# The output projection of three pooling groups: seven block products in the place of eight

## The chip, the cores and the metric

The kernel runs on one core of a Trainium2 chip. The metric is the device time of one execution in microseconds (us); the number that counts is the median of several runs.

## The reference

The reference is a two-part network in float32 on 1024 tokens of width 1024. The part that matters here is the pooling mixer of the second block, which has four groups of 512 channels:

```python
def pool_mixer(h, w_in, w_group, scale, w_out):
    u, z = jnp.split(h @ w_in, 2, axis=-1)
    p = causal_multiscale_pool(u).reshape(B, S, N_POOL_GROUPS, GROUP_WIDTH)
    y = jnp.einsum('bsgc,gcd->bsgd', p, w_group).reshape(B, S, A_WIDTH_2) * scale
    return (y * jax.nn.silu(z)) @ w_out
...
    x = x + gate[:, None, :] * y
```

After the mixer, the keys and values of an attention layer are made from the new x: an RMS norm over x, a modulation, and a product with w_kv. That stage is called the key stage here.

## The kernel before

Activations lie transposed: 128 channels on the partitions, 1024 tokens along the free dimension, so x is 8 tiles (xT, tile o). TensorE multiplies in a 32-bit format that rounds its inputs, so each float32 operand is split in a high part (a rounded copy) and a low part (the rest), and each product of a 128x128 weight block with 512 tokens is three matmuls: high by high, high by low, low by high (`product`, L705, L706, L708). The high part of a weight block is a cast on ScalarE (`group_high`, L2884), the low part a subtraction on GpSimd (`group_low`, L1658). Weights come in strips by SyncE's DMA queue (`load_group_half`, L1434) into `raw`, two slots of two halves, and each half is loaded again once the low part made from it is there.

The pooling groups g = 1, 2, 3 run one after the other. In each, work goes by forms: a form is four 128x128 weight blocks, split into one of four places of split_hi and split_lo (form p uses place p % 4, so the split of form p waits until TensorE has done form p - 4). A group has 40 forms:

- Forms 0 to 27, the input projection, in four quads of seven (`pool_quad`). Each quad does a 2x2 block product with seven products in the place of eight (the Strassen-Winograd scheme): sums of weight blocks are made on GpSimd (L1672, L1674, L1677, L1679), sums of the token blocks were made once, and VectorE adds the seven results up (L3655 to L3675). A form is 12 matmuls of 512 tokens. The low part of the seventh form of each quad is made by VectorE (`plain_low`, L3684); the last half strip of the quad's weights can be overwritten only after it.
- Forms 28 to 31, the group's own square matrix, one tile of 1024 tokens each, 24 matmuls. VectorE multiplies the result with the gate (`gate_product`, L3589), ScalarE casts the high part (L2834), VectorE makes the low part (`gate_low`, L3594).
- Forms 32 to 39, the output projection, one tile of x each: 4 blocks of channels by 1024 tokens, 24 matmuls. VectorE adds each to x (`residual`, L3607). In the last group ScalarE squares and splits each finished tile of x for the key stage (L481, L564), and VectorE adds the squares and makes the low parts between the residuals (L488, L581).

The order on every engine is the order in the program. ScalarE waits in `group_high` for the place to come free, GpSimd waits for ScalarE's cast, SyncE waits for the low part. Tiles 6 and 7 of x lie in DRAM while a group runs, and ScalarE's queue brings them back (`x_pair_d`).

## Time and profile before

| | us |
|---|---|
| median of 3 runs (2353.84 to 2354.54) | 2354.03 |
| the profiled execution | 2353.32 |
| its span in the profile | 2351.4 |
| TensorE busy in the span | 2324.9 |
| VectorE busy | 1537.1 |
| ScalarE busy | 859.8 |
| GpSimd busy | 1255.9 |

Around the span lie 1.9 us. TensorE's granted clock is at full speed throughout (0.999). A matmul's entry is 0.39 us long, but matmuls overlap: what one costs in a stream is the distance from its start to the next one's. Groups 1 to 3 run from 1513 to 1946 us.

### The profile page before, as it was taken

How to read it: one execution, taken by the hardware profiler on the slowest of the kernel's cores; microseconds unless marked ns; L12 is line 12 of the kernel's file. 1: busy time of each engine (PE TensorE's matmuls, PEld its weight loads, DVE VectorE, ACT ScalarE, POOL GpSimd, SP SyncE). 2: the span in 40 equal slices, each digit the busy share in tenths (PEclk: the TensorE clock that was granted, in tenths of full speed). 3: DMA queues.
4: the chain of work that ended last, by engine and by line, in shares of the span. 5: the costliest groups of instructions: out<-in, count | busy, mean ns of one | idle time of the engine just before them, and what ended most of it. 6: DMA issues, size and time to landing. Idle time of an engine off the chain costs nothing.

```text
span 2351.4 us, 32286 instructions
## 1 busy us (share of the span) xinstructions
PE 2324.9 (99%) x11585; PEld 1943.6 (83%) x11585; DVE 1537.1 (65%) x1839; ACT 859.8 (37%) x1596; POOL 1255.9 (53%) x724
## 2 busy tenths in 40 slices
PE   9999999999999999999999999999999999999998
PEld 7888789888888888888888888788878788889887
DVE  7825555524578777877877777774672967147885
ACT  5212555512543222222222443122231244157773
POOL 4533954143135666676777424573754733467743
PEclk9999999999999999999999999999999999999999
DMA  6511001031011333333332211112121123210034
GB/s 220 157 45 50 19 19 37 1 117 54 10 42 50 117 125 125 117 124 125 117 123 63 63 45 45 59 57 73 54 81 62 58 67 110 79 37 25 22 112 139
DMA packets 67420, 179.08 MB, mean 76 GB/s; under 512 B 7010, under 2 KB 13924, under 8 KB 65200
## 3 DMA queue, kind: packets, MB, share of 16 engines
q1 hardware_dynamic: 57840, 148.03, 19.3%
q10 hardware_dynamic: 9104, 27.51, 3.5%
q0 software_dynamic: 368, 2.10, 0.5%
q8 instruction: 68, 1.11, 0.2%
q14 instruction: 40, 0.33, 0.0%
HBM read 161.84 MB, written 15.77 MB: 76 GB/s over the span
## 4 chain that ended last, share of the span: by engine, by line
PE 76%; DVE 6%; issue 4%; POOL 2%; ACT 1%; DMA 0%; POOLq 0%; DVEq 0%; ACTq 0%; SPq 0%
PE ps L705 21%; PE ps L706 21%; PE ps L708 21%; PE ps L855 4%; PE ps L833 3%; PE ps L843 2%; DVE trail L3538 1%; PE ps L2410 1%; POOL split_lo L1658 1%; PE ps L2426 1%; ACT p L956 1%; PE ps L2395 1%; PE ps L2396 1%; PE ps L2425 1%; PE ps L509 0%
## 5 line engine op out<-in xcount | busy, mean ns | idle before, releaser
L705 PE MATMUL ps<-h_hi,split_hi 128*128 128x512 f32 x1546 | 607.2, 393 | 3.4 <-DVE h_lo L3220 1.3
L706 PE MATMUL ps<-h_lo,split_hi 128*128 128x512 f32 x1546 | 601.9, 389 | 0.0
L708 PE MATMUL ps<-h_hi,split_lo 128*128 128x512 f32 x1546 | 536.5, 389 | 0.0
L1516 POOL TENSOR_TENSOR split_hi<-raw,cf 128x1024 fp32r<-128x1024 f32 x64 | 125.2, 1956 | 427.8 <-PE ps L708 373.2
L705 PEld LDWEIGHTS ps<-h_hi,split_hi 128*128 128x128 f32 x1546 | 290.9, 188 | 63.9 <-issue 2.2
L708 PEld LDWEIGHTS ps<-h_hi,split_lo 128*128 128x128 f32 x1546 | 290.9, 188 | 61.0
L706 PEld LDWEIGHTS ps<-h_lo,split_hi 128*128 128x128 f32 x1546 | 291.2, 188 | 56.3 <-issue 0.2
L1605 POOL TENSOR_TENSOR split_lo<-raw,split_hi 128x512 fp32r<-128x512 f32 x144 | 232.9, 1635 | 193.9 <-ACT split_hi L2723 193.4
L1658 POOL TENSOR_TENSOR split_lo<-raw,split_hi 128x512 fp32r<-128x512 f32 x84 | 128.1, 1534 | 179.2 <-ACT split_hi L2884 179.2
L2723 ACT CAST split_hi<-raw 128x512 fp32r<-128x512 f32 x144 | 86.7, 622 | 283.9 <-PE ps L708 204.0
L1518 POOL TENSOR_TENSOR split_lo<-raw,split_hi 128x1024 fp32r<-128x1024 f32 x64 | 178.4, 2787 | 5.0
L705 PE MATMUL ps<-act_hi,split_hi 128*128 128x512 f32 x320 | 125.5, 392 | 1.5 <-DVE xT L3443 1.4
L706 PE MATMUL ps<-act_lo,split_hi 128*128 128x512 f32 x320 | 124.8, 390 | 0.0
L3760 DVE CUSTOM_DVE_ANT_0 p<-ps,swa_bias,sink_row 128x256 f32<-128x256 f32 (+1 forms) x128 | 54.6, 464 | 102.8 <-PE ps L2396 102.3
L2884 ACT CAST split_hi<-raw 128x512 fp32r<-128x512 f32 x96 | 58.2, 620 | 138.8 <-PE ps L708 128.4
L3443 DVE TENSOR_TENSOR xT<-xT,ps 128x1024 f32<-128x1024 f32 x72 | 87.4, 1214 | 30.6 <-PE ps L708 30.5
L3313 DVE SCALAR_TENSOR_TENSOR ada_acc<-ada_raw,cact,ada_acc 128x1024 f32<-128x1024 f32 x56 | 102.6, 1832 | 0.8
L705 PE MATMUL ps<-p_hi,split_hi 128*128 128x512 f32 x256 | 99.9, 390 | 0.5 <-DVE pool_tmp L3665 0.5
L706 PE MATMUL ps<-y_lo,split_hi 128*128 128x512 f32 x256 | 99.8, 390 | 0.0
L708 PE MATMUL ps<-act_hi,split_lo 128*128 128x512 f32 x320 | 98.7, 390 | 0.0
L705 PE MATMUL ps<-sum_hi,split_hi 128*128 128x512 f32 x240 | 93.7, 390 | 0.3 <-ACT quad_tmp L2748 0.3
L706 PE MATMUL ps<-sum_lo,split_hi 128*128 128x512 f32 x240 | 93.6, 390 | 0.0
(508 smaller groups left out, 5213.2 us busy)
## 6 DMA issues: line engine op xcount, KB each, us to landing
raw<-in_strips SPq DMA_DIRECT2D x208, 256.0 KB, 2.8
raw<-in_strips SPq DMA_DIRECT2D x86, 512.0 KB, 3.4
ada_raw<-in_ada SPq DMA_DIRECT2D x64, 512.0 KB, 3.7
memw_raw<-in_mem_strips SPq DMA_DIRECT2D x8, 512.0 KB, 6.1
xT<-in_xT ACTq DMA_DIRECT2D x4, 1024.0 KB, 8.1
x_spill_d<-xT ACTq DMA_DIRECT2D x1, 3584.0 KB, 10.1
xT<-x_spill_d ACTq DMA_DIRECT2D x2, 1792.0 KB, 9.9
out_T<-out_sb SPq DMA_DIRECT2D x13, 256.0 KB, 2.2
```

The lines of the kernel that those rows point to most:

```text
L705: pe.matmul(acc[:, a:b], w_hi, hi[:, a:b], start=first, stop=False)
L706: pe.matmul(acc[:, a:b], w_hi, lo[:, a:b], start=False, stop=False)
L708: mm = pe.matmul(acc[:, a:b], w_lo, hi[:, a:b], start=False, stop=last)
L833: mm = pe.matmul(at[:, lo:hi], q, k, start=j == 0, stop=j == len(group) - 1)
L855: mm = pe.matmul(o, a["pt"][:, w % 4, j * P:(j + 1) * P], unit["values"][b0 + j], start=b0 + j == 0, stop=b0 + j == nblk - 1)
L1516: pool.tensor_tensor(hi, raw[:, r, :], ones[:, 0:1].to_broadcast([P, D]), ALU.mult).then_inc(hi_split, 1)
L1518: pool.tensor_tensor(lo, raw[:, r, :], rows(hi), ALU.subtract).then_inc(split_ready[r], 1)
L1605: pool.tensor_tensor(form_tiles(split_lo, p), src, rows(form_tiles(split_hi, p)), ALU.subtract).then_inc(form_ready, 1)
L1658: pool.tensor_tensor(group_tiles(split_lo, p), src, rows(group_tiles(split_hi, p)), ALU.subtract).then_inc(form_ready, 1)
L2723: act.copy(form_tiles(split_hi, p), src).then_inc(form_hi, 1)
L3313: dve.scalar_tensor_tensor(out=ada_acc[:, :], in0=ada_raw[:, r, :], scalar=cact[:, k:k + 1], in1=ada_acc[:, :], op0=ALU.mult, op1=ALU.add) ...
L3443: dve.tensor_tensor(xT[:, o, :], xT[:, o, :], pair(2 + o % 2), ALU.add).then_inc(ffn_res, 1)
```

## The change

In groups 1 to 3 the output projection is done in two quads of seven forms (`out_form`), each for four tiles of x, in the place of eight forms. The 4 channel tiles of the group are two pairs, the tokens two halves, and a quad's four tiles of x two pairs; a form is two parts (one for each tile of a pair), each of 2 blocks by 512 tokens, 12 matmuls in all. A group has 46 forms. Some forms add onto a PSUM bank that was read before (`start=i in (0, 1, 3)`).

New on each engine, per group:

- GpSimd: the low parts of 12 forms and four sums in each quad (`out_forms`), where there were 8 low parts. The second form of a quad is the low part of a sum of both halves of the second strip.
- ScalarE: 14 weight casts in the place of 8, the casts of the token sums in halves (`out_high`, `neg_high_tile`), in group 3 the key stage's squares and splits at other places (`key_square`).
- VectorE: the token differences (`first_difference`, `neg_two`, `neg_three`, `neg_four`), their low parts, 28 additions of 512 tokens to x (`out_sum`) in the place of 8 of 1024, and the low part of each quad's seventh form (`plain_low`). In group 3, the squares' additions and the low parts of the key stage.
- In groups 1 and 2 the token sums lie where half of the tiles 0 to 5 of h was. Those halves are saved to DRAM in group 1 (`h_keep_d`), and in the next group they come back on ScalarE's DMA queue (`h_fetch`) and ScalarE rounds them again (`h_round`, six casts), for which the sixth and seventh form wait.
- SyncE loads the last half strip of a quad after its sixth and seventh form are split (`load_out`). The strips of the output weights are packed in another order.
- The loops over groups on TensorE, GpSimd and SyncE are written out.

```diff
+            def load_out(g, quad):
+                for i, d in ((2, 0), (3, 1), (4, 2), (6, 3)):
+                    if d == 3:
+                        group_split(sp, g, out_form(quad, 5))
+                    group_split(sp, g, out_form(quad, i))
+                    load_group_half(g, 12 + 2 * quad + d // 2, d % 2)
...
+            def out_forms(g, quad):
+                j, at = 10 + 2 * quad, out_form(quad, 0)
+                group_half(pool, g, j, 0)
+                group_low(g, at, OUT_SOURCE[0])
+                group_half(pool, g, j + 1, 0)
+                group_half(pool, g, j + 1, 1)
+                pool.tensor_tensor(pool_form, a21, a22, ALU.add).then_inc(form_sum, 1)
+                group_low(g, at + 1, OUT_SOURCE[1])
+                summed(g, 4 + quad, 1)
+                pool.tensor_tensor(a21, a21, a11, ALU.subtract).then_inc(form_sum, 1)
+                group_split(pool, g, at + 1)
+                pool.tensor_tensor(pool_form, a11, pool_form, ALU.subtract).then_inc(form_sum, 1)
+                group_low(g, at + 2, OUT_SOURCE[2])
...
+                pool.tensor_tensor(pool_form, a12, pool_form, ALU.add).then_inc(form_sum, 1)
+                for i in range(3, 6):
+                    group_low(g, at + i, OUT_SOURCE[i])
...
+            def out_quad(g, quad):
+                for i in range(7):
+                    p = out_form(quad, i)
+                    group_split(pe, g, p)
+                    if quad == 0:
+                        if i in (2, 4, 6):
+                            neg_lower(pe, g, i)
+                        else:
+                            gate_lower(pe, g, {0: 1, 1: 3, 3: 5, 5: 6}[i])
...
+                        elif i in OUT_AFTER:
+                            out_read(pe, g, 14 * quad + 2 * OUT_AFTER[i] + part + 1)
...
+                product(pe, bank(OUT_BANKS[quad][OUT_BANK[i]][part]), slot,
+                        [(w + 2 * part + kk, *out_token(g, i, kk)) for kk in range(2)], HALF, start=i in (0, 1, 3), skip=True)\
...
+            def out_tokens_made(g):
+                first_difference(g, 0)
+                first_difference(g, 1)
+                gates_low(g, 3, y_lo[:, 0:2, t1], gates[:, 0:2, t1], y_hi[:, 0:2, t1])
+                gate_step(g, 2).then_inc(pool_g, 1)
...
+                neg_two(g, 0)
+                neg_three(g, 0)
+                difference_low(g, 0)
+                neg_four(g, 0)
+                neg_low(g, 2, 0)
+                gate_step(g, 3, t2).then_inc(pool_g, 1)
...
+                neg_two(g, 1)
+                neg_three(g, 1)
+                difference_low(g, 1)
+                gate_step(g, 3, t1).then_inc(pool_g, 1)
...
+                neg_four(g, 1)
+                neg_low(g, 2, 1)
+                out_sum(g, 0, 0, 0)
+                out_sum(g, 0, 0, 1)
+                gates_low(g, 4, y_lo[:, 2, :], gated_tile(2), gated_hi_tile(2))
+                gates_low(g, 6, y_lo[:, 3, t1], gated_tile(3)[:, t1], gated_hi_tile(3)[:, t1])
+                out_sum(g, 0, 1, 0)
+                out_sum(g, 0, 1, 1)
+                neg_low(g, 3, 0)
+                neg_low(g, 3, 1)
+                out_sum(g, 0, 2, 0)
+                out_sum(g, 0, 2, 1)
+                gates_low(g, 5, y_lo[:, 3, t2], gated_tile(3)[:, t2], gated_hi_tile(3)[:, t2])
+                out_sum(g, 0, 3, 0)
+                out_sum(g, 0, 3, 1)
+                neg_low(g, 4, 0)
+                neg_low(g, 4, 1)
+                out_sum(g, 0, 4, 0)
+                out_sum(g, 0, 4, 1)
+                plain_low(g, 4)
...
+                for quad in range(2):
+                    for i in range(7) if quad else (5, 6):
+                        for part in range(2):
+                            out_sum(g, quad, i, part)
+                            if quad and i == 3 and part == 1:
+                                plain_low(g, 5)
+                            if g == POOL_GROUPS - 1 and quad and i == 5 and part == 1:
+                                key_low(4)
+                        if g == POOL_GROUPS - 1 and quad and i < 4:
+                            key_low(i)
...
+            key_low(5)
+            for k in range(3, 7):
+                norm_add(dve, n_kv, k)
+            key_low(6)
+            norm_add(dve, n_kv, 7)
+            key_low(7)
```

## Rows read from the trace of the kernel before

**Rows 1.** The page: the span and each engine's busy time (share) and instructions.
```profile
span 2351.4 us, 32286 instructions
PE 2324.9 (99%) x11585; PEld 1943.6 (83%) x11585; DVE 1537.1 (65%) x1839; ACT 859.8 (37%) x1596; POOL 1255.9 (53%) x724
```

**Rows 2.** Waits of TensorE, 1655 to 1797 us (group 2): total, times, longest.
```profile
PE ps L705 <- DVE pool_tmp L3665: 0.5, 1, 0.5
PE ps L705 <- POOL split_lo L1658: 0.3, 1, 0.3
```

**Rows 3.** Stretches: start:end, length, busy PE, PEld, DVE, ACT, POOL (instructions), clock.
```profile
1655.00:1732.00 77.00, 76.71 (x335) 62.32 (x334) 57.39 (x51) 20.01 (x32) 57.21 (x35) 1.00 0.20 68
...
1758.50:1802.00 43.50, 43.50 (x193) 36.04 (x192) 12.62 (x10) 7.00 (x10) 15.96 (x12) 1.00 0.16 54
1902.60:1946.10 43.50, 43.50 (x193) 36.04 (x193) 30.55 (x22) 19.33 (x21) 14.18 (x7) 1.00 0.20 66
```

**Rows 4.** Timeline of TensorE: start, length, line; group 2's output projection begins and ends.
```profile
1758.53 0.39 PE L705 MATMUL ps<-y_hi,split_hi 128*128 128x512 f32 x1
...
1802.05 0.39 PE L705 MATMUL ps<-h_hi,split_hi 128*128 128x512 f32 x1
```

**Rows 5.** Timelines of VectorE and GpSimd around tiles 2 and 3 of group 2.
```profile
1753.26 1.28 DVE L3589 SCALAR_TENSOR_TENSOR gates<-ps,cols,gates 128x1024 f32<-128x1024 f32 x1 [2.39 <-PE ps L708]
1754.47 1.87 DVE L3594 TENSOR_TENSOR y_lo<-gates,y_hi 128x1024 fp32r<-128x1024 f32 x1
1758.73 1.28 DVE L3589 SCALAR_TENSOR_TENSOR gates<-ps,cols,gates 128x1024 f32<-128x1024 f32 x1 [2.40 <-PE ps L708]
...
1753.97 1.29 POOL L1658 TENSOR_TENSOR split_lo<-raw,split_hi 128x512 fp32r<-128x512 f32 x1 [4.17 <-ACT split_hi L2884]
```

**Rows 6.** Timeline of VectorE: half-width steps in an input quad.
```profile
1669.30 0.69 DVE L3657 TENSOR_TENSOR pool_tmp<-pool_tmp,ps 128x512 f32<-128x512 f32 x1 [4.67 <-PE ps L708]
1669.90 0.68 DVE L3684 TENSOR_TENSOR split_lo<-raw,split_hi 128x512 fp32r<-128x512 f32 x1
```

**Rows 7.** Timeline of the DMA issues, and the half strips' time to landing (groups 1 to 3).
```profile
1670.75 0.33 SPq L1434 DMA_DIRECT2D raw<-in_strips  x1
...
DMA to landing us min/median/max: 2.5/2.8/4.4
```

**Rows 8.** Timelines of GpSimd and ScalarE: sums, a cast and low parts of a quad's weights.
```profile
1793.32 1.28 POOL L1672 TENSOR_TENSOR small<-raw 128x512 f32<-128x512 f32 x1
1794.68 1.29 POOL L1674 TENSOR_TENSOR raw<-raw 128x512 f32<-128x512 f32 x1
1797.51 1.29 POOL L1658 TENSOR_TENSOR split_lo<-small,split_hi 128x512 fp32r<-128x512 f32 x1 [1.54 <-ACT split_hi L2884]
...
1796.81 0.62 ACT L2884 CAST split_hi<-small 128x512 fp32r<-128x512 f32 x1 [4.82 <-PE ps L708]
```

**Rows 9.** Timeline of VectorE: a norm addition, a low part, the last residual.
```profile
1945.37 1.23 DVE L488 TENSOR_TENSOR sq_sum_kv<-sq_sum_kv,sq_kv 128x1024 f32<-128x1024 f32 x1
1946.51 2.92 DVE L581 SCALAR_TENSOR_TENSOR h_lo<-xT,gmod,h_hi 128x1024 fp32r<-128x1024 f32 x1
1949.35 1.27 DVE L3607 SCALAR_TENSOR_TENSOR xT<-ps,adav,xT 128x1024 f32<-128x1024 f32 x1
```

**Rows 10.** Timelines of GpSimd, ScalarE and TensorE at the beginning of the key stage.
```profile
1946.41 1.94 POOL L1516 TENSOR_TENSOR split_hi<-raw,cf 128x1024 fp32r<-128x1024 f32 x1 [5.64 <-PE ps L708]
1948.43 3.27 POOL L1518 TENSOR_TENSOR split_lo<-raw,split_hi 128x1024 fp32r<-128x1024 f32 x1
...
1950.66 1.06 ACT L481 ACTIVATE sq_kv<-xT 128x1024 f32<-128x1024 f32 x1 [4.28 <-DVE xT L3607]
1951.63 1.13 ACT L564 ACTIVATE h_hi<-xT,gmod 128x1024 fp32r<-128x1024 f32 x1
...
1946.16 0.39 PE L705 MATMUL ps<-h_hi,split_hi 128*128 128x512 f32 x1
1953.13 1.92 PE L509 MATMUL ps<-cf,sq_sum_kv 128*128 128x1 f32 x16
```

More of the change, by code:

```diff
@@ L384, in group_at @@
         def group_at(p):
-            return p % 4 // 2, 4 * (p % 2)
+            return GROUP_SLOT[p] // 2, 4 * (GROUP_SLOT[p] % 2)
         def group_tiles(tensor, p):
@@ L473, in norm_place @@
         def norm_place(n, k):
+            if n["places"] is not None:
+                return n["places"][k]
             return n["sq_sum"] if k == 0 else n["sq"] if n["other"] is None or k % 2 else n["other"]
@@ L3685, in plain_low, with key_low, gate_step @@
                    .then_inc(plain_ready, 1)
+            def key_low(k):
+                split_low(dve, sp_kv, KV_ORDER[k])
+            def gate_step(g, t, tok=slice(0, T), tile=None):
+                group_through(dve, g, GROUP_TILE_AT + t)
+                dve.wait_ge(pool_sz, 4 * g + t + 1)
+                return dve.scalar_tensor_tensor(out=gated_tile(t)[:, tok], in0=group_pair(g, t)[:, tok], scalar=col("ascale", 4 * g + t),
+                                                in1=gated_tile(t)[:, tok], op0=ALU.mult, op1=ALU.mult)
@@ new lines, in first_difference, with gates_low, neg_two @@
+            def first_difference(g, t):
+                link(gate_step(g, t))
+                dve.tensor_tensor(gated_tile(t)[:, t2], gated_tile(t)[:, t2], gated_tile(t)[:, t1], ALU.subtract).then_inc(pool_g, 1)
+            def gates_low(g, n, out, src, hi):
+                gate_high(dve, g, n)
+                dve.tensor_tensor(out, src, rows(hi), ALU.subtract).then_inc(pool_ylo, 1)
+            def neg_two(g, kk):
+                dve.tensor_tensor(neg_full(g, 2, kk), gated_tile(kk)[:, t2], gated_tile(2 + kk)[:, t2], ALU.subtract).then_inc(neg_sum, 1)
@@ new lines, in difference_low, with out_sum @@
+            def difference_low(g, t):
+                gates_low(g, 1 + t, y_lo[:, t, t2], gated_tile(t)[:, t2], y_hi[:, t, t2])
+            def out_sum(g, quad, i, part):
+                p = out_form(quad, i)
+                if part:
+                    group_through(dve, g, p)
+                else:
+                    dve.wait_ge(pool_tile, 6 + 14 * (g - 1) + 7 * quad + i + 1)
+                if quad == 1 and i == 0 and part == 1:
+                    dve.wait_ge(x_again[0], 16 * g)
+                if i in (3, 4, 5):
+                    out_read(dve, g, 14 * quad + 2 * {3: 0, 4: 1, 5: 2}[i] + part + 1)
+                o, tok = 4 * quad + 2 * part + (i in OUT_SECOND), out_tokens[i in OUT_LATE]
+                dve.scalar_tensor_tensor(out=xT[:, o, tok], in0=bank(OUT_BANKS[quad][OUT_BANK[i]][part]), scalar=adav[:, 16 + o:17 + o],
+                                         in1=xT[:, o, tok], op0=ALU.mult, op1=ALU.add).then_inc(pool_res, 1)
```

282 lines of the change are left out of this document (202 added, 80 removed).

## The prediction

> **What bounds the kernel now.** The page comes first: TensorE is busy for 2324.9 of 2351.4 us and VectorE for 65% [rows 1]. Then the waits of TensorE over group 2: 0.8 us in 142 us [rows 2]. So the time in this stage is the number of matmuls times the distance of two starts, and nothing that is taken from another engine can gain. The table of stretches says how much room the others have: in the input quads, which already run by seven products, VectorE and GpSimd are both busy for 57 of 77 us; in the output projection VectorE has 12.6 of 43.5 us and GpSimd 16.0, in group 3 VectorE 30.6 with the key stage's work [rows 3]. The change spends this room. What decides is whether its steps come in time, so the rest is a schedule. It counts from the first matmul of the output projection (1758.53 in the trace) as zero.
>
> **What is saved.** The projection of group 2 runs from 1758.53 to 1802.05, 43.52 us for 192 matmuls, 0.227 us each [rows 4]. Two quads of seven forms of 12 are 168 matmuls, 38.1 us. 24 fewer in each of three groups save 3 x 5.44 = 16.3 us, all on the path. (The Trainium skill, "TensorE: Matmul & The Clock Gate", section "Back-to-back issue gap", gives about 216 ns for an isolated 512-column matmul; by that it would be 15.6 us. The trace has 227.)
>
> **VectorE in the first quad.** A half-width VectorE step costs 0.60 us from start to start and 0.68 until its result is there, whether it reads PSUM or SBUF twice [rows 6]. But steps that read SBUF twice and GpSimd's steps exclude each other: GpSimd's low part runs from 1753.97 to 1755.26, the y_lo begun at 1754.47 ends at 1756.34, 1.08 after GpSimd, and takes 1.87; the gate step, which reads PSUM, takes 1.28 always [rows 5]. (This is the shared port pair of the Trainium skill, "SBUF — State Buffer", section "Who interferes with whom": an exclusive lock against two SBUF inputs. The trace agrees; by the rule alone the waits below come out the same.)
>
> Before zero: tile 2 can be gated from -5.2. Form 34's low part is on GpSimd from -4.56 to -3.27 as today's third output form is [rows 5], and the fourth weight sum follows. neg_two, neg_three, difference_low, neg_four and neg_low come then; the first two each wait for one of GpSimd's steps, and the last ends at 0.9 where without that it would be done before tile 3's result at 0.2. From 0.95 on VectorE has, up to the end of `plain_low(g, 4)`, 26 half-width steps: 2 gate halves, 14 that read SBUF twice (gates_low of tile 2 counts two), 10 out_sums. 26 x 0.60 is 15.6, and 0.4 for the steps that wait for the one ahead of them and for the last result: 16.95. On the way GpSimd makes the low parts of forms 35, 36 and 37, held back by ScalarE's casts to 4.4, 6.8 and 9.2: neg_low waits for the first (1.25), gates_low hardly for the second (0.1), the next gates_low for the third (1.3). Together 2.65, so the block is there at **19.6**. TensorE meanwhile waits 1.1 us for difference_low(1) ahead of form 1, 1.1 for neg_low and out_sum ahead of form 2, 0.9 for gates_low ahead of form 3 and 0.1 to 0.3 ahead of form 4, and reaches form 6 at 19.8 in the place of 16.3. VectorE is the bound of this quad.
>
> **The chain behind it.** The last half strip of the second quad can only be loaded after that `plain_low`; here it is needed for the second form, in the input quads only for the third. SyncE issues 0.15 us after the low part's end and the half lands 2.8 later [rows 6, 7]: 22.6. Sum 1.3, cast 0.7, low part 1.4 [rows 8]: form 1 is ready at 26.0. GpSimd then makes two more sums at 1.37 from start to start, then cast 0.7 and low part 1.4: form 2 is ready at 30.8, 8.2 after the landing. TensorE can have form 2 at 24.5 if it never waits. It gets it at 30.9, and five forms of 2.72 follow: **44.5**. So the stage of 43.5 becomes 44.5, with 6.4 us of waits against 5.44 saved.
>
> Bounds of the wait: `plain_low` stands behind the out_sum of form 4's second part, which TensorE ends at 13.6 at the earliest. So it ends no earlier than 15.1, the half lands at 18.0, form 2 is ready at 26.3: at least **1.8 us** of wait per group. If VectorE never meets GpSimd and starts at 0.2, `plain_low` ends at 16.3, and the wait is 3.0. I take 6.4, as the lock is seen in this very place in the rows. In the second quad VectorE has out_sums alone and catches up; the forms behind form 2 have their weights just in time.
>
> **GpSimd, ScalarE, DMA.** GpSimd gets 12 more steps per group, 16 us beside 16 of 43.5 [rows 3]: hidden, but for the chain. ScalarE's casts are 0.62 each [rows 8]; the six h_round at a next group's start are 1.0 each, and by the same count the cast of form 4 is ready about 1.2 us before its turn, which costs nothing. They push VectorE's first_products by some 2 us, which its 20 idle us of 77 in the quads take up [rows 3]; bounds 0 to 2 us for each of two groups; I take 0. The half tiles' saving and return is 3 MB out and 2 x 3 MB back beside a DMA share of 0.2 [rows 3] and is asked for early: 0. Loops written out: 0, since TensorE shows no idle time at the turns of today's loop.
>
> **Group 3 and the key stage.** Today the finished tiles of x come 5.44 us apart, and squares and splits hide between. TensorE goes on at 1946.16 without a gap, through 5 tiles to the norm's sum at 1953.13 [rows 10]. After the change tiles 4 and 6 are final one form before the end, 5 and 7 at the end. In the second quad VectorE waits for ScalarE's splits inside key_low: out_sum of form 4 comes late for form 6 and a low part meets key_low, 1.4 us. Counted from TensorE's end of the projection, VectorE has key_low(4) at 2, waits there or behind it for GpSimd's strip split, which holds the second read for 1.9 and 2.2 us (today h_lo takes 2.92 beside it [rows 9, 10]), then norm_add(2), two out_sums, key_low(5), four norm_adds of 1.15 [rows 9], key_low(6): 15.0. TensorE has seven tiles of 1.36 us each: it waits 2.2 us ahead of the sixth, 4.6 ahead of the seventh. The norm's sum and the eighth tile then need no wait. **+6.8 us**; without the lock +4, at least +3.
>
> **Sum.** 2353.3 - 16.3 + 3 x 6.4 + 1.4 + 6.8 = **2364.4**. The profiled execution is 0.7 under the median; that is within the rounding of these terms.
>
> **Rivals.**
> The locks bite little (B): VectorE's two-input steps fall between GpSimd's. For it: GpSimd has only four steps in the first quad. Against it: both are released by the same ends of forms. -16.3 + 9.0 + 0.5 + 4.0: 2350.5.
> VectorE keeps up (C), the case on the other side: `plain_low` ends right behind form 4's results, so that only the chain's floor of 1.8 us is left. It decides at 15.1 us; each us later costs a us per group. For it: the floor is fixed by program order; against it: 26 steps must then fit in 14.9 us, 0.57 each, below the 0.60 of the rows. -16.3 + 5.4 + 3.0: 2345.4.
> Spill-over (D): VectorE's delay at the next group's start is not taken up; its means are the tail of the quads, with 0.5 us of wait there today [rows 2]. 3 us more in two groups and 2 more at the key stage: 2372.
> The products are not saved: no, 24 matmuls per group are gone from the program.
>
> **How the numbers follow.** The forecast (A) has 0.54 and spans 2357 to 2369; B 0.20; C 0.16; D 0.10. About 0.2%, 4.7 us, is what a measurement of this kernel can tell from no change: faster is below 2349.3, slower above 2358.7. C and a fourth of B make faster 0.21; three fourths of B and a part of A's lower end same 0.22; slower 0.57. The range takes in C's and D's values: 2345 to 2372.
>
> **What would show it.** TensorE's waits in the three output stages: about 19 us if A holds, 9 in B, 5 in C; most on the split_lo of the second quad's second and third form, with a releaser on GpSimd, and on VectorE in the first quad. The load of the second quad's last half is issued about 20 us after the first output matmul; if at 15, C holds. The two-input steps of VectorE should be 1.0 to 1.9 us long where GpSimd works. Between the last output matmul and the norm's sum lie 16 us in the place of 7. I am wrong if SyncE's load comes early though VectorE is late, or if the gain is eaten elsewhere.

## The result, and the profile of the changed kernel

The changed kernel takes 2386.57 us (median of 4 runs, 2380.01 to 2387.64) against 2354.28 for the kernel before beside it: a ratio of 1.0131, 95% interval 1.0112 to 1.015. It is slower, as forecast, but by 32 us and not by 10, and outside the range. The profiled execution took 2385.95 us; its span is 2384.1 (2351.4 before). One run of one kernel below, the one with thinned additions, had a granted clock of 0.62 and took 3469 us; it is left out.

The page of the changed kernel, and the waits of TensorE in group 2's output stage (1763 to 1808 us), then in its input stage (1657 to 1763 us): who waited for whom, total, times, longest.

```profile
span 2384.1 us, 32018 instructions
PE 2323.7 (97%) x11513; PEld 1932.5 (81%) x11513; DVE 1602.9 (67%) x1956; ACT 895.0 (38%) x1651; POOL 1305.1 (55%) x759
```

```profile
PE ps L766 <- POOL split_lo L1725: 3.0, 3, 1.5
PE ps L766 <- DVE xT L3910: 1.0, 2, 0.8
PE ps L766 <- DVE y_lo L3877: 0.8, 1, 0.8
```

```profile
PE ps L766 <- POOL split_lo L1725: 5.3, 5, 1.5
```

TensorE's busy time hardly moved (2324.9 before, [rows 1]), though 72 matmuls, some 16 us, are gone: others ran at half the clock, and around each wait the entries, 0.39 us and more long, don't overlap. So a wait costs a little more than its entry says: the 168 matmuls of group 2's output stage take 38.1 us at 0.227 each, its six waits are 4.8 in sum, and the stage takes 44.8. The table of stretches puts them in order: group 2's input and output stages, group 3's, and the stretch from the last output matmul to the norm's sum. Its columns are start:end, length, then each engine's busy time, the granted clock, DMA share and GB/s.

```profile
1657.57:1763.20 105.63, 100.35 (x434) 80.69 (x432) 71.52 (x69) 39.25 (x56) 75.74 (x50) 1.00 0.26 83
1763.20:1807.96 44.76, 39.92 (x170) 30.97 (x168) 33.00 (x45) 11.96 (x20) 20.38 (x15) 1.00 0.27 88
1807.96:1915.50 107.54, 100.53 (x434) 80.69 (x432) 82.04 (x73) 39.02 (x56) 82.51 (x50) 1.00 0.25 81
1915.50:1962.67 47.17, 41.25 (x169) 30.73 (x168) 39.24 (x48) 19.75 (x27) 23.10 (x14) 1.00 0.21 63
1962.67:1981.13 18.46, 11.86 (x44) 8.57 (x43) 16.18 (x14) 9.46 (x9) 4.30 (x2) 0.79 0.15 55
```

Before, an output stage was 43.5 us long [rows 3, 4]; the input stages, from a group's start to its first output matmul, were 100.5 and 100.6; and 6.97 us lay between the last output matmul and the norm's sum [rows 10]. So the 32.7 us between the two spans are:

| where | us |
|---|---|
| ahead of group 1's output stage | -1.7 |
| three output stages (44.75, 44.76, 47.17) | +6.1 |
| input stages of groups 2 and 3 | +5.2, +6.9 |
| from the last output matmul to the end of the kernel (405.2 before, 421.4 now) | +16.2 |

The output stages are nearly what the prediction said (it had +4.3). The next two lines, 28 us, hold the miss: 12 us that it had put at nothing, and 9 us more than it had counted behind the projection.

The first line comes from TensorE's clock, not from the change. The profile of the kernel before isn't at full speed throughout: behind 16 one-column products, with no wait over 0.1 us ahead of them, the granted clock is at its half for 3.4 us (the last 3.5 us of the span are at the half too). A matmul then starts 0.427 us behind the one ahead of it in the place of 0.227, which costs 1.7 us in all.

```profile
1355.85 1.92 PE L509 MATMUL ps<-cf,sq_sum 128*128 128x1 f32 x16
```

```profile
1355.00:1358.00 3.00, 2.93 (x22) 1.00 0.48 175
1358.00:1361.50 3.50, 3.50 (x10) 0.51 0.00 0
```

Of the 14 profiled executions of this study, which do the same work there, eight have this fall and reach group 1's first output matmul at 1613.6 to 1614.9 us; six, that of the changed kernel among them, don't have it and reach it at 1611.8 to 1613.0.

**The input stages.** The timelines of ScalarE, its DMA queue (ACTq) and GpSimd at the start of group 2 in the changed kernel, and the time to landing of the half strips issued from 1640 to 1680 us:

```profile
1652.34 1.93 ACTq L3032 DMA_DIRECT2D h_plain<-h_keep_d  x4
1654.37 1.15 ACT L3006 CAST split_hi<-raw 128x512 fp32r<-128x512 f32 x2 [1.41 <-issue]
...
1665.69 0.89 ACTq L3032 DMA_DIRECT2D h_plain<-h_keep_d  x2
1666.62 0.48 ACTq L3047 DMA_DIRECT2D x_pair_d<-xT  x1
1667.14 1.04 ACT L3037 CAST h_hi<-h_plain 128x1024 fp32r<-128x1024 f32 x1 [0.84 <-issue]
```

```profile
1660.33 1.29 POOL L1759 TENSOR_TENSOR small<-raw 128x512 f32<-128x512 f32 x1 [2.64 <-DMA raw<-in_strips]
```

```profile
DMA to landing us min/median/max: 2.5/3.0/7.2
```

The first four of the six returning transfers, 512 KB each, are issued right in front of the group's start. The half strip that GpSimd's first sum needs is issued at 1653.76, behind three of them and 0.02 us ahead of the fourth, and lands 6.4 us later; before, the longest was 4.2 in this stretch. (The 7.2 is another half strip, issued at 1668.21 behind the last two returning transfers and one of 1 MB for tiles 6 and 7 of x.) GpSimd's sum starts 2.64 us late, and TensorE waits for its low parts 1.1, 0.9 and 0.3 us, and twice 1.5 later.

**The key stage.** Granted clock and load of TensorE in stretches of 10 us (length, busy, clock, DMA share, GB/s), and its first matmul behind each wait:

```profile
1960.00:1970.00 10.00, 9.89 (x42) 1.00 0.38 125
1970.00:1980.00 10.00, 3.51 (x11) 0.67 0.03 10
1980.00:1990.00 10.00, 10.00 (x41) 0.50 0.00 1
1990.00:2000.00 10.00, 10.00 (x35) 0.63 0.17 52
```

```profile
1972.08 0.50 PE L766 MATMUL ps<-h_hi,split_hi 128*128 128x512 f32 x1 [2.00 <-DVE h_lo L641]
1978.40 0.80 PE L766 MATMUL ps<-h_hi,split_hi 128*128 128x512 f32 x1 [4.50 <-DVE h_lo L641]
1981.13 3.41 PE L569 MATMUL ps<-cf,sums_f 128*128 128x1 f32 x16
```

The waits are the two forecast ones (2.0 and 4.5 us; forecast 2.2 and 4.6). What was not counted stands beside them: the granted clock goes from 1.00 (2.4 GHz) to 0.50 (1.2 GHz) and is back at 1.00 only 23.9 us later, at 1997.4. Before, it was 1.00 in the whole key stage. The work behind the sum shows the price. From the norm's sum to the end the kernel before takes 398.3 us with 11 key tiles still to make, the changed one 403.0 with nine, 2.7 us less work: 7.4 us lost, and 1.4 more in the seventh tile, made at half clock.

That is one execution. The four of the changed kernel have a mean granted clock of 0.993 to 0.996, and the fastest, 2380.01 us, has the 0.996; the kernel before has 0.998 or 0.999. Some kernels of the experiments below keep the first wait and all or most of the second, and show how much the fall can differ (one profiled execution each; the last row is a kernel nearly without these waits):

| kernel | the two waits, us | clock at its half for, us | from the norm's sum to the end, us |
|---|---|---|---|
| changed | 2.00, 4.50 | 23.9 | 402.9 |
| return moved to SyncE | 1.99, 3.88 | 17.1 | 399.5 |
| return thinned | 1.99, 3.62 | 17.1 | 399.4 |
| low part early | 1.99, 4.68 | 10.2 | 398.8 |
| low part early, changed head | 1.99, 4.67 | 3.4 | 396.1 |
| additions thinned | 1.07, 0.47 | 0 | 395.4 |

So the waits are nearly the same, and their price behind the sum is anything from 0.5 to 7.4 us. The difference of two spans, from one execution each, holds this difference too; below, what a change is worth is read stage by stage.

### The profile page after: what moved, and what is told of

Read it like the earlier page. It is cut to its first block, busy times and chain, and to the rows that moved or that the text cites. A ratio compares the mean times of both kernels' runs of the same rounds, so it can differ in the third digit from the quotient of the medians.

```text
span 2384.1 us, 32018 instructions
## 1 busy us (share of the span) xinstructions
PE 2323.7 (97%) x11513; PEld 1932.5 (81%) x11513; DVE 1602.9 (67%) x1956; ACT 895.0 (38%) x1651; POOL 1305.1 (55%) x759
## 3 DMA queue, kind: packets, MB, share of 16 engines
q1 hardware_dynamic: 57840, 148.03, 19.6%
## 4 chain that ended last, share of the span: by engine, by line
PE 67%; DVE 9%; POOL 5%; issue 4%; ACT 3%; DMA 1%; ACTq 0%; DVEq 0%; POOLq 0%; SPq 0%
PE ps L766 18%; PE ps L769 17%; PE ps L767 17%; PE ps L916 4%; PE ps L894 3%; PE ps L904 2%; POOL split_lo L1725 2%; DMA raw<-in_strips 1%; PE ps L2525 1%; DVE xT L3910 1%; POOL small L1764 1%; PE ps L2541 1%; POOL small L1759 1%; DVE y_lo L3877 1%; POOL raw L1761 1%
## 5 line engine op out<-in xcount | busy, mean ns | idle before, releaser
L766 PE MATMUL ps<-h_hi,split_hi 128*128 128x512 f32 x1594 | 627.7, 394 | 16.6 <-DVE h_lo L641 8.6
L767 PE MATMUL ps<-h_lo,split_hi 128*128 128x512 f32 x1594 | 621.1, 390 | 0.0
L769 PE MATMUL ps<-h_hi,split_lo 128*128 128x512 f32 x1594 | 556.2, 390 | 0.0
L766 PEld LDWEIGHTS ps<-h_hi,split_hi 128*128 128x128 f32 x1594 | 300.6, 189 | 83.3 <-DVE h_lo L641 8.3
L769 PEld LDWEIGHTS ps<-h_hi,split_lo 128*128 128x128 f32 x1594 | 300.4, 188 | 63.4
L1672 POOL TENSOR_TENSOR split_lo<-raw,split_hi 128x512 fp32r<-128x512 f32 x144 | 232.0, 1630 | 193.7 <-ACT split_hi L2838 191.8
L2838 ACT CAST split_hi<-raw 128x512 fp32r<-128x512 f32 x144 | 87.1, 623 | 282.1 <-PE ps L769 203.2
L1725 POOL TENSOR_TENSOR split_lo<-raw,split_hi 128x512 fp32r<-128x512 f32 x78 | 118.9, 1537 | 115.1 <-ACT split_hi L3006 115.0
L3617 DVE TENSOR_TENSOR xT<-xT,ps 128x1024 f32<-128x1024 f32 x72 | 87.4, 1214 | 30.8 <-PE ps L769 30.7
L769 PE MATMUL ps<-sum_hi,split_lo 128*128 128x512 f32 x240 | 93.4, 389 | 0.0
L951 DVE TENSOR_REDUCE small<-ps 128x1 f32<-128x256 f32 (+7 forms) x96 | 61.7, 644 | 38.1 <-PE ps L894 37.5
L548 DVE TENSOR_TENSOR sq_sum<-sq_sum,sq 128x1024 f32<-128x1024 f32 (+2 forms) x47 | 70.3, 1496 | 24.6 <-ACT sq L541 24.3
```

The source lines that it names most:

```text
L766: pe.matmul(acc[:, a:b], w_hi, hi[:, a:b], start=first, stop=False, skip_group_check=skip)
L767: pe.matmul(acc[:, a:b], w_hi, lo[:, a:b], start=False, stop=False, skip_group_check=skip)
L769: mm = pe.matmul(acc[:, a:b], w_lo, hi[:, a:b], start=False, stop=last, skip_group_check=skip)
L1672: pool.tensor_tensor(form_tiles(split_lo, p), src, rows(form_tiles(split_hi, p)), ALU.subtract).then_inc(form_ready, 1)
L1725: pool.tensor_tensor(group_tiles(split_lo, p), src, rows(group_tiles(split_hi, p)), ALU.subtract).then_inc(form_ready, 1)
L2838: act.copy(form_tiles(split_hi, p), src).then_inc(form_hi, 1)
```

## The experiments

Three theories were to be told apart. **1**: the late `plain_low(g, 4)` delays the second quad (the prediction's). **2**: the return of the kept tokens costs the input stages' 12 us; 2a because of where it is issued, 2b because of its 3 MB. **3**: the fall of the clock comes from the key stage's waits. The rival to all three: one of them is the same loss seen twice, or a fourth cause is left.

### The low part made early

```diff
                 out_sum(g, 0, 2, 1)
+                plain_low(g, 4)
...
                 out_sum(g, 0, 4, 1)
-                plain_low(g, 4)
```

> Edit to the changed kernel: in the first output quad VectorE makes the low part of the plain block (plain_low(g, 4)) behind the second out_sum of form 2, two places of the order earlier, and nothing else moves. Theory 1 (the chain of last half strip, two weight sums and two low parts behind that plain block sets the output stage): the low part ends some 15.4 us after the first output matmul in the place of 19.8, the load is issued there, and each group's output stage (44.8 us in the changed kernel) falls to 40.5 to 41.5, over three groups 10 us. Rival (VectorE as a whole is the bound of the stage, the order inside it is nothing): the stage stays at 44 to 45 us. Nothing is expected of the waits at the start of the next group (5 to 7 us each in groups 2 and 3) nor of the two waits at the key stage (2.0 and 4.5 us). If the low clock behind the key stage comes from those two waits alone, it stays as it is and the kernel takes about 2376; if it also needs the waits of the groups ahead, it goes too and the kernel takes about 2366.

2375.15 us (2374.37 to 2376.57), ratio 1.0097 (1.008 to 1.0114), against 1.0131. Waits of TensorE in group 2's output stage, then GpSimd's first sum of the second quad's weights, in the changed kernel and in this one:

```profile
PE ps L766 <- POOL split_lo L1725: 1.0, 1, 1.0
PE ps L766 <- DVE xT L3910: 1.0, 2, 0.8
PE ps L766 <- DVE y_lo L3877: 0.8, 1, 0.8
```

```profile
1786.25 1.29 POOL L1737 TENSOR_TENSOR small<-raw 128x512 f32<-128x512 f32 x1 [6.08 <-DMA raw<-in_strips]
```

```profile
1781.75 1.30 POOL L1737 TENSOR_TENSOR small<-raw 128x512 f32<-128x512 f32 x1 [1.75 <-DMA raw<-in_strips]
```

The second quad's waits are gone, and the three output stages take 42.0, 42.0 and 43.3 us in the place of 44.8, 44.8 and 47.2: 9.3 us come back, 2.7 in each of the first two groups, where 40.5 to 41.5 us a stage had been expected. Theory 1 holds for the output stages. The span is 11.5 us shorter, but that is not 3.8 a group: 4.1 us lie behind the projection, where the clock was down for 10.2 us and not 23.9 behind the same two waits, and the stretch ahead of group 1's output stage is 1.6 longer, with the fall at 1358 us. The first quad's 2.8 us of waits stay, and so do the waits of the input stages.

The view puts the third of these waits down to GpSimd's low part. That is done at 1774.03 us in the changed kernel, and TensorE goes on at 1774.68, right behind VectorE's y_lo, which ends at 1774.58; all four waits of the first quad are VectorE's.

### The return of the tokens, thinned and moved

The first of the two returns and rounds again only 16 of 512 columns:

```diff
-act.dma_start(h_plain[:, NK * low + a:NK * low + a + 2, HALF:T], h_keep_d[:, low, a:a + 2, :])
+act.dma_start(h_plain[:, NK * low + a:NK * low + a + 2, HALF:HALF + 16], h_keep_d[:, low, a:a + 2, 0:16])
-act.copy(of[:, a:a + 2, HALF:T], h_plain[:, NK * low + a:NK * low + a + 2, HALF:T])
+act.copy(of[:, a:a + 2, HALF:HALF + 16], h_plain[:, NK * low + a:NK * low + a + 2, HALF:HALF + 16])
```

> Edit to the changed kernel: of the half tiles of h that ScalarE's queue brings back in the next group only 16 of 512 columns are loaded and rounded again, so the output is wrong behind group 1; every wait, issue and instruction stays. Theory 1 (the 3 MB that come back fill the DMA engines, and the half strip of weights that TensorE's third form of the group waits for lands 6.5 us after its issue in the place of 2.8): the half strips land in under 3.5 us, the waits on GpSimd's low parts at the start of groups 2 and 3 go, and each group's stretch from first input matmul to first output matmul falls from 105.6 to about 101. Rival (these waits come from the late low part of the plain block of the second output quad and from the four DMA issues in front of ScalarE's casts, which stay): the half lands sooner but the waits keep 1 to 2 us per group, and the stretch stays above 103.

The second keeps all bytes and all rounding, and has SyncE issue them:

```diff
                 load_out(g, 1)
+                if g < POOL_GROUPS - 1:
+                    for m, done in ((2, h_again), (3, h_again), (4, h_kept)):
+                        a = NEG_T[m]
+                        if m == 4:
+                            group_through(sp, g, out_form(1, 6))
+                        for low in range(2):
+                            sp.dma_start(h_plain[:, NK * low + a:NK * low + a + 2, HALF:T], h_keep_d[:, low, a:a + 2, :]).then_inc(done, 16)
```

> The changed kernel, with one thing moved: the loads that bring the kept tokens back (3 MB for each of groups 2 and 3) are issued on SyncE's queue instead of ScalarE's, the first four behind the last half strip of the group, the last two when TensorE has read the group's last form. Their bytes, and ScalarE's re-rounding, stay. Theory 2a (what costs is that ScalarE issues them, late, with its casts behind them): the waits of TensorE between 0 and 14 us from the start of groups 2 and 3 (1.1, 0.9 and 0.3 us, then 1.5 to 2.4 at 30 us) go, a group is 4 to 6 us shorter, and the kernel takes 2374 to 2378. Theory 2b (what costs is 3 MB beside the weights on the same 16 DMA engines): the half strips still land in up to 7 us, the waits stay within 1 us in sum, and the kernel takes 2383 to 2387. Earlier issue could also push the second quad's half strips: then the last output stage waits of groups 1 and 2 grow by 1 to 2 us.

The thinned one took 2373.22 us in its one run, the moved one 2373.79 (2370.76 to 2374.5), ratio 1.0084 (1.0068 to 1.0101). In the thinned one ScalarE still issues the four transfers in 1.93 us, and GpSimd's first sum has no wait ahead of it:

```profile
1654.39 1.93 ACTq L3032 DMA_DIRECT2D h_plain<-h_keep_d  x4
```

```profile
1659.70 1.29 POOL L1759 TENSOR_TENSOR small<-raw 128x512 f32<-128x512 f32 x1
```

In the moved one:

```profile
1657.77 1.29 POOL L1766 TENSOR_TENSOR small<-raw 128x512 f32<-128x512 f32 x1 [0.76 <-DMA raw<-in_strips]
```

```profile
DMA to landing us min/median/max: 2.5/2.7/4.8
```

The distance from one group's first output matmul to the next one's tells it best, in us:

| kernel | 1 to 2 | 2 to 3 |
|---|---|---|
| before | 144.0 | 144.1 |
| changed | 150.4 | 152.3 |
| low part early | 148.0 | 149.6 |
| return moved to SyncE | 147.0 | 146.1 |
| return thinned | 145.8 | 145.4 |
| low part early, return moved (the kernel with three repairs, below) | 144.1 | 143.5 |
| low part early, return thinned (the kernel with three thinnings, below) | 143.1 | 142.6 |

Take the last two rows against the third. The return with its rounding costs 4.9 and 6.9 us (from the unrounded distances); 3.9 and 6.1 of it go when the same 3 MB are issued elsewhere. The profiles of the later kernels say how firm that is. The input stages of groups 2 and 3 take 105.2 to 106.0 and 107.5 to 108.6 us in the four profiles in which ScalarE's queue brings all the bytes back, 101.7 to 103.1 and 101.3 to 104.2 in the five in which SyncE's does, 101.0 and 100.6 in the two with thinned return, 100.5 and 100.6 in the kernel before. So theory 2a holds. What is left for the 3 MB as such and for the rounding, 0.7 to 3.6 us a stage, differs by as much from one execution to the next. Not all that 2a forecast came: the waits of 1.1, 0.9 and 0.3 us are gone, but group 2 still has one of 1.15 and one of 1.52 later on. The Trainium skill, "DMA: Bandwidth & Descriptors", section "Issuing engines are not separate DMA queues", says that all issuing engines end on the same 16 DMA engines and that another one saves only the time to issue. The trace agrees: 1.93 us of issue for four transfers leaves ScalarE. But this time is not what the return cost: the thinned kernel keeps it and is 0.5 us from the kernel before in group 2's input stage. The gain must be order, then: the strip is issued at 1654.60, ahead of the transfers, and no longer among them. That is by elimination; the re-rounding was not taken alone.

### The key stage's additions thinned

```diff
-dve.tensor_tensor(n["sq_sum"], n["sq_sum"], norm_place(n, k), ALU.add)
+part = slice(0, 16 if n["places"] is not None else n["width"])
+dve.tensor_tensor(n["sq_sum"][:, part], n["sq_sum"][:, part], norm_place(n, k)[:, part], ALU.add)
```

> Edit to the changed kernel: VectorE's seven additions of squares at the key stage take 16 of 1024 columns, so the norm of the key stage is wrong; their order and waits stay. Theory 1 (TensorE's two waits of 2.0 and 4.5 us there are VectorE's chain of low parts and additions, and these waits drop TensorE's clock): the additions fall from about 1.2 to 0.15 us, the wait ahead of the sixth tile goes, that ahead of the seventh falls under 1.5 us, the granted clock stays at 1.00 behind it, and the kernel takes 2368 to 2373 in the place of 2386. Rival (the clock falls because of all the waits of the output stages and group starts before): the waits go but the clock still falls, and the kernel takes about 2380.

2374.70 us (2373.76 to 2375.34, 3 runs), ratio 1.0094 (1.0074 to 1.0114), some 2 us above the range expected. The waits fall from 2.00 and 4.50 to 1.07 and 0.47, and the clock stays up:

```profile
1970.00:1980.00 10.00, 8.47 (x46) 1.00 0.19 52
1980.00:1990.00 10.00, 10.00 (x57) 1.00 0.14 53
```

From the norm's sum to the end it takes 395.4 us with nine tiles to make: with the 2.7 us of the two missing tiles 398.1, the 398.3 of the kernel before. Behind the projection 14.3 us come back: 5.0 are waits, 8.9 the clock (7.5 behind the norm's sum, 1.4 in the seventh tile). That speaks for theory 3. The span is only 12.2 us shorter, since the rest of this execution is 2.1 slower. The clock fell in it twice for 3.4 us elsewhere, at 1358.4 and at 1843.1, the second time behind a wait of 2.45 us in group 3's input stage; behind the wait of 2.40 there in the changed kernel it did not.

### A wait of that length in the kernel before

```diff
+            for _ in range(6):
+                link(dve.tensor_tensor(pooled[:, 0, EDGE:], xT[:, 0, :], xT[:, 1, :], ALU.add))
             norm_add(dve, n_kv, NK - 1)
```

> The kernel before, with six idle additions of 1024 columns (1.2 us each) on VectorE ahead of the last norm addition of the key stage: TensorE, which doesn't wait there now, waits some 6 to 7 us for the norm's sum, once. Theory 3 (a gap of this length of itself brings the granted clock down for a while): granted clock 0.5 to 0.7 in the 20 us behind the gap, and 6 us of wait plus 6 to 9 us at the lower clock: 2365 to 2369. Rival (the clock falls only because the stretch ahead, with its waits, had already been thin): the clock stays at 1.00 and the kernel takes 2358 to 2360.

And with three of them in the place of six:

> The kernel before with three idle additions instead of six ahead of the last norm addition: TensorE waits some 3.7 us (7.4 with six). With six it cost 12.8 us, 7.4 of wait and some 5.5 of clock. If a gap of 3 to 4 us brings the clock down as the longer one does: 3.7 + 4 to 6, 2360 to 2362, granted clock below 0.8 behind it. If a gap of this length doesn't: 2356 to 2357 and a clock of 1.00.

With six, TensorE waits 7.37 us, once, and the kernel takes 2365.33 (2362.53 to 2366.36; before: 2352.5), +12.8, of which 5.5 are not the wait. With three it waits 3.58, and takes 2359.32 (2357.69 to 2362.27, 7 runs; before: 2352.93), +6.4, of which 2.8 are not the wait. These are medians; the single runs with three lie 1.2 to 5.8 us above the wait, the fastest with a mean clock of 0.998, the two slowest with 0.996. The granted clock around the wait with three, in the profiled execution (2361.95 us):

```profile
1950.00:1960.00 10.00, 6.42 (x30) 0.80 0.16 52
1960.00:1970.00 10.00, 10.00 (x46) 0.69 0.01 2
1970.00:1980.00 10.00, 10.00 (x45) 1.00 0.18 52
```

The clock is at its half from 1956.0 us, while TensorE still waits, for 10.2 us (with six from 1954.8, for 10.2 as well). Nothing else was changed, so a wait of 3.6 us in a stretch that is full otherwise brings the clock down, and adds about three quarters of its own length by the medians. The rival, that it takes a stretch already thinned, falls.

### The three thinnings together

> The three thinnings of the runs before in one kernel: the low part made early, 16 of 512 columns of the kept tokens returned and rounded again, 16 of 1024 columns added in the key stage's seven norm additions. It leaves out most of the return and of the additions. If the three causes are separate and are all, the spans saved (11.5, 12.8 and 12.2 us) add up: 2384.1 - 36.5 = a span of 2347.6, a time of 2347 to 2352. If two of them are the same loss seen twice, or a fourth cause is left, it stays above 2356.

2352.34 us (2350.05 to 2354.31, 10 runs) against 2352.5: ratio 0.9997 (0.9987 to 1.0007), span 2350.0. The three add up to 34.1 us of span where 36.5 were expected. The spans of the first two hold some 4 us each of a shorter fall of the clock, so the stages are the better check (us saved against the changed kernel):

| stretch, and what was thinned | alone | with all three |
|---|---|---|
| three output stages, low part early | 9.3 | 8.8 |
| input stages of groups 2 and 3, return | 11.5 | 11.5 |
| behind the projection, additions | 14.3 | 13.9 |

So they are three causes, each worth the same beside the others, and together they undo the loss against the kernel before. The fourth that is left is the forecast one: even with most of the return and of the additions left out, the kernel is only level with the one before, as the output stages take 127.9 us in the place of 130.6, where 3 x 168 matmuls in a row would take some 114. Most of the 16.3 us saved still goes to the first quad's waits and what hangs on them.

### Repairs that keep the work

The low part early, the return on SyncE's queue, and a new order of the key stage:

```diff
-                    if g == POOL_GROUPS - 1 and out_form(1, 2) <= p < out_form(1, 6):
-                        key_square(p - out_form(1, 2))
+                    if g == POOL_GROUPS - 1 and out_form(1, 1) <= p < out_form(1, 5):
+                        key_square(p - out_form(1, 1))
...
+            for k in range(4, NK):
+                key_low(k)
+            for k in range(4, NK):
+                norm_add(dve, n_kv, k)
...
+            product(pe, pair(2), S_KV % 2, h_pieces(KV_ORDER), before=as_split(pe, sp_kv))
...
+            norm_sum(pe, n_kv)
...
+            strip_part(S_KV + 1, pair(3), range(1), free=h_free)
+            norm_spread(pe, n_kv)
```

> The changed kernel with three repairs, its whole computation kept: the low part of the first output quad's last form is made behind the third form's sums instead of behind the fifth's; the kept tokens come back on SyncE's queue; in the key stage ScalarE's first four squares come one form earlier, the last four high parts come ahead of their squares, VectorE makes the last four low parts ahead of the last four additions, and TensorE takes the norm's sum behind all eight key tiles, with one tile of the next strip behind it. If my three causes hold, it gives back 11 us in the output stages, 4 to 6 a group in the return (by theory 2a of the run beside this one; 0 by 2b), and in the key stage one wait of 1 to 4 us instead of 2.0 and 4.5, and the granted clock stays at 1.00 there: 2351 to 2358 by 2a, 2360 to 2368 by 2b. If the clock falls all the same, 8 us more. Rival: the changed order of the key stage takes the cover from the stage behind it, where VectorE makes the next eight tiles at 2.5 us each: new waits of 1 to 3 us at its fifth tile.

2362.68 us (2359.73 to 2364.97), ratio 1.0045 (1.0028 to 1.0062), against 1.0131: by the ratios 20 of the 31 us are back, by the spans 26 of 33. That is 5 us above the range that 2a gave with the clock up, and inside it with the 8 us that it added for a fall. The two key waits have become 0.98 and 3.03, and the clock still falls, to its half for 6.8 us:

```profile
1959.33 2.73 PE L569 MATMUL ps<-cf,sums_f 128*128 128x1 f32 x16 [3.03 <-DVE sums_f L548]
```

```profile
1960.00:1970.00 10.00, 10.00 (x49) 0.66 0.00 1
```

Then the gap was filled with two tiles of the next strip (2.7 us of TensorE's work):

> The kernel with the three repairs (2362.7; its norm's sum starts at 1959.3 us after a wait of 3.0, the granted clock falls to 0.66 in the next 10 us, and the fifth tile of the strip after the next waits 1.1 at 1986.5), with one thing moved: TensorE makes two tiles of the next strip (2.7 us) ahead of the norm's sum, not behind it; same work, same result. If what the key stage loses is the gap and the clock it brings down, TensorE doesn't wait at the norm's sum, the clock stays at 1.00 there, and the kernel takes 2356 to 2358. Rival: behind the key stage VectorE's chain is the bound, from the norm's last addition by the spread rows to the eight next tiles at 2.5 us each. Then the clock stays up at the norm's sum, but the gap turns up again at the fifth tile as a wait of 3 to 5 us, the clock falls there instead, and the kernel takes 2360 to 2363.

2360.93 us (2358.32 to 2363.92), ratio 1.0031 (1.0021 to 1.0042). TensorE's waits around the norm's sum and at the strip after the next:

```profile
1960.39 1.92 PE L569 MATMUL ps<-cf,sums_f 128*128 128x1 f32 x16 [0.35 <-DVE sums_f L548]
...
1984.61 0.50 PE L766 MATMUL ps<-h_hi,split_hi 128*128 128x512 f32 x1 [0.54 <-DVE h_lo L638]
1987.12 0.50 PE L766 MATMUL ps<-h_hi,split_hi 128*128 128x512 f32 x1 [0.85 <-DVE h_lo L638]
```

```profile
1960.00:1970.00 10.00, 9.65 (x50) 0.67 0.00 1
1970.00:1980.00 10.00, 10.00 (x46) 0.82 0.14 55
```

Neither theory is right as written. The gap is gone from the norm's sum, and yet the clock falls to 0.67, where TensorE had waited 0.97 at 1951.6 and 0.35 here and made 16 one-column products. The time is the rival's, 2360 to 2363, but not by its waits, which are 1.4 us in sum and not 3 to 5. That this kernel is faster than the one with three repairs isn't shown: the intervals of their ratios overlap, and so does that of the next one.

The next kernel has TensorE sum the last square itself; the one after that changes VectorE's order at the head of the output stage, on top of the early low part; a third has all of it. The first and the third don't compute the right norm: eight sums are open in one bank of PSUM at once. The Trainium skill, "PSUM — Partial Sum Buffer", section "The four PSUM rules", says that the start of a second one makes the first one's next matmul overwrite; no run here shows that by itself. Their instructions and waits are those of the full work.

```diff
+            for t in range(T // P):
+                pe.matmul(n_kv["columns"][:, t:t + 1], kv_squares[NK - 1][:, t * P:(t + 1) * P], ones[:, 0:1],
+                          start=True, stop=False, skip_group_check=True)
```

> The kernel with the three repairs (span 2357.9, its norm's sum 3.0 us late, granted clock 0.66 in the 10 us behind it), with the seventh norm addition taken off VectorE's tail: TensorE sums the eighth square itself, by eight more products of 128x128 by one column, while VectorE makes the sixth addition. Theory 3 (a gap of some 3 us brings the clock down for some 5 us): TensorE now waits under 1 us, the clock stays at 1.00, and the kernel is 4 to 6 us shorter, 2356 to 2359. If the clock falls from the wait of 1.0 us ahead of the fifth key tile as well, only 1 to 2 us: 2360 to 2362.

> The kernel with the low part of the last form made early (2375.2), with VectorE's order at the head of the first output quad changed, the same work: the low part of the first tile's first half is made in the gap in which VectorE waits for the second tile's product, ScalarE's copy of the first halves is made in two, and the low part that the second form waits for comes one step earlier. In that kernel TensorE waits 0.85, 0.79, 0.97 and 0.2 us ahead of the second to fifth form of each group's first quad. If VectorE's steps are the bound there, 1 to 1.7 us of the 2.8 go in each of three groups: 2370 to 2372. If it is GpSimd's and ScalarE's chain for the weights, nothing goes: 2374 to 2376.

> Everything together, whole computation: low part early, tokens back on SyncE's queue, the key stage's order with TensorE's own sum of the last square, and the changed order at the head of the first output quad. From the two runs beside it: 4 to 6 us below the kernel with three repairs by the key stage, and 3 to 5 more by the head of the quad: 2350 to 2355, so within 0.2 per cent of the kernel before, or just below it.

With the last addition gone: 2360.09 us (2356.16 to 2362.65), ratio 1.0029 (1.0016 to 1.0042). The time is that of the second case. No wait at the norm's sum is left, only 1.0 ahead of the fifth tile, and the clock is at its half all the same from 1965.0 us for 10.2 us, behind 32 one-column products:

```profile
1960.16 1.84 PE L2405 MATMUL ps<-cf,last_tmp 128*128 128x1 f32 x16
1961.95 1.95 PE L2409 MATMUL ps<-cf,sums_f 128*128 128x1 f32 x16
```

With the changed head: 2369.6 us (2367.2 to 2377.03) against 2375.15. But the waits of the first quad only moved, 0.64, 1.39 and 0.63 in the place of 0.84, 0.76 and 1.00, 2.7 against 2.8 in sum. The stages are 0.5 us shorter each (41.5 in the place of 42.0), not the 1 to 1.7 expected; of the rest between the two profiles, 2.8 us are a fall of the clock of 3.4 us in the place of 10.2 behind the same key waits. The intervals of the two ratios (1.0066 to 1.0097 here) overlap. With everything: 2356.54 us (2353.13 to 2366.31, 11 runs), ratio 1.0022 (1.0012 to 1.0032), above the 2350 to 2355 expected. No version beat the kernel before.

## Why the prediction was right, and where it was wrong

**What bounds, what is saved**: right. 24 matmuls a group are gone, and an output stage of 168 takes 42.0 us in groups 1 and 2 once the low part comes early.

**The first quad and the chain behind it**: right, in size and in place. Forecast waits of 1.1, 1.1, 0.9 and 0.1 to 0.3 us; measured 0.84, 0.76, 1.03 and 0.24. `plain_low(g, 4)` was to end at 19.6 and ended at 20.3. GpSimd's low part of form 2 was to be ready at 30.8; it was at 31.0. The stage was to take 44.5 and took 44.75. The early low part, which took 2.7 us off the stages of groups 1 and 2 and 3.9 off group 3's, is the proof for the chain; of the first quad's waits it is the rows alone. VectorE's two-input steps did grow beside GpSimd's as forecast (3.22 us for a low part of 1.27 at 1965.16).

**Group 3 and the key stage, the waits**: right, nearly in size. 2.0 and 4.5 us stand against 2.2 and 4.6; group 3's output stage is 2.4 us longer than the others, against 1.4.

**GpSimd, ScalarE, DMA: the first step that failed.** "The half tiles' saving and return is 3 MB out and 2 x 3 MB back beside a DMA share of 0.2 and is asked for early: 0." It measured 12 us, 5.2 and 6.9. The share of 0.2 is a mean over 77 us. What counted was the few us at a group's start: three transfers of 512 KB are issued ahead of the half strip on which GpSimd's first sum, and with it the third form, hangs, and a fourth right behind it. The row to read was the landing time of the strips [rows 7], with 2 MB put beside one of them: at the 300 to 435 GB/s that the busy slices of this stretch show, 2 MB take some 5 to 7 us, an estimate (the strip landed after 6.4). The bound of the same paragraph, 0 to 2 us for each group, was for ScalarE's casts alone. The rival "spill-over" had the right place, the beginning of the next groups, but another carrier, VectorE's delay, and 3 us a group in the place of 5 to 7.

**The clock: the second step.** The sum counts every wait at its own length. From 1973.5 us, in the second of the waits of 2.0 and 4.5 us, TensorE's clock was at 1.2 GHz for 23.9 us, and that cost about 9 us more in the profiled execution (8.9 by the kernel with thinned additions; less, and differing, in the others with these waits). The trace of the kernel before did show a fall and its price, 0.2 us for each matmul at the half, at 1358 us, without a wait; the mean of 0.999 was taken for full speed throughout. A wait of 6.8 us in a kernel that has only short ones should have brought a case of its own, with a price from both sides.

**The sum.** 2364.4 + 12.1 + 9.3 = 2385.8, against 2385.95 in the profiled run. That it closes so well is luck in part: the output stages took 1.8 us more than forecast and the stretch ahead of them 1.7 less, and another execution of this kernel, at a higher mean clock, took 2380. "The gain is eaten elsewhere" was among the things that would make the prediction wrong; it had no price and no chance.

## What to carry to other kernels

A transfer that is "hidden" must be costed at the moment at which it is issued, beside the load that the critical chain waits for in those microseconds, and not against the mean share of the queues. In a kernel whose matmul engine never waits, a new wait of some 3 us costs more than its length, since the clock can go down with it; here 1.75 times by the medians, 1.3 to 2.6 times in single runs. One profile can't price such a fall: look at the mean clock of every run, and compare stage by stage. And when a change takes matmuls away from a stage, list what else must fit into the shorter stage: here VectorE's chain at the end, which no reordering tried here brought back to where it had been.

## What was not expected of the hardware

- One wait of 3.58 us between full stretches brings the granted clock to its half for 10.2 us (0.80 and 0.69 over 20 us) and costs 2.8 us beyond itself by the medians; one of 7.37 costs 5.5 beyond itself.
- The same pair of waits, 2.0 and 4.5 to 4.7 us, was followed by 23.9, 10.2 and 3.4 us at the half clock in three profiled executions.
- The clock fell with shorter waits too: for 10.2 us behind waits of 0.97 and 0.35 us and 16 one-column products, for 10.2 behind one of 1.00 and 32 such products, and in the kernel before for 3.4 us behind 16 such products and no wait over 0.1, which the same work shows in eight of 14 executions. With 1.07 and 0.47 and 16 products it stayed at 1.00, twice. What tells these apart is open. The kernels in this region also spread more from run to run (2353 to 2366 for the last one, whose slowest run has the lowest mean clock, 0.995) than the kernel before (2351 to 2356).
- A half strip of 256 KB that lands in 2.7 us alone needs 6.4 among four transfers of 512 KB, and 7.2 behind two of these and one of 1 MB.
